# Three in eight dot products of two expert blocks moved from VectorE to GpSimd and ScalarE, in a decoder layer with a product-key expert FFN

## The chip, the cores and the metric

One Trainium2 chip, one core of it. The metric is the device time of one execution of the whole kernel in microseconds.

## The reference

One decoder layer on 1024 tokens of width 1024, in float32. The first part (combined projection, dilated attention, a gated recurrence, cross-attention, gated merge, layer norm) is not touched by the change. The second part is a product-key expert FFN (PEER): each token picks 8 x 16 = 128 of 16384 experts, takes the dot product of its row with each expert's row of `u_tab`, applies GELU and the gate, and sums the experts' rows of `v_tab` with these weights.

```python
q = jnp.einsum('bsd,dk->bsk', h, w_q).reshape(b, s, PEER_HEADS, 2, PEER_DHALF)
sc = jnp.einsum('bshpk,hpnk->bshpn', q, sub_keys).astype(jnp.float32)
...
top, pos = lax.top_k(cand, PEER_TOPK)
idx = jnp.take_along_axis(cidx, pos, axis=-1)
gate = jax.nn.softmax(top, axis=-1)
...
def block(args):
    xt, it, gt = args
    act = jax.nn.gelu(jnp.einsum('td,ted->te', xt, u_tab[it]), approximate=False)
    return jnp.einsum('te,ted->td', gt * act, v_tab[it])
```

Then `h = LN(alpha*h + ffn)`.

## The kernel before

Each engine has its own program, written out by hand in order; semaphores tie them. The tokens are in 8 blocks of 128 (`NBLK`), one token per partition. The dots of block 0 are done earlier, beside the second half of the attention part (`e_rows`, L1766). The stage that the change touches starts at about 1920 us of the span and has these pieces:

- **Gathers.** For block n and slot k (0 to 127), GpSimd waits until the ring slot k mod 8 of `u_ring` is free and issues an indirect DMA of one expert row per token, 512 KB in all (L859).
- **Dots.** `dot(n, k)` on VectorE (L2097) waits for that gather, multiplies the row by the tokens' residual rows, which TensorE has raised into PSUM as `h1_up` (`raise_h1`, L1197), and sums along the row into `coef[:, k]`, in one instruction and an accumulator read. Its semaphore `u_dots` frees the ring slot.
- **Coefficients.** After all 128 dots of a block: `gelus` on ScalarE (L1564), `coefficients` on VectorE (L2105, times the gate), `turn` on TensorE (transpose), `turn_out` on ScalarE.
- **Weights by expert.** For 32 groups of four tokens: `hots` on VectorE (L2080, two comparisons of 128x512 whose operands are both in SBUF), `scale` on ScalarE (four copies), `pair` on TensorE, `pair_out` on ScalarE (into `table`). `hots` may run two groups ahead of `pair`.
- **Values.** `values_of(p, i)` on TensorE (L1215): in pass p, tile i of 64, a tile of 128 rows of `v_tab` (512 KB, a ring of 4 filled from Sync's queue) is multiplied with the table of one or two blocks.

The order: a prologue of 32 sub-steps does `hots(0, sub)` and one dot of block 1 each. Then 9 passes of 64 tiles. In tiles 0 to 27 (`DOT_TILES`) of pass p VectorE does what is left of block p+1's dots, at tile 28 its coefficients, and in tiles 32 to 63 `hots(p+1, ..)` and the first 64 dots of block p+2, two a tile. How many dots stand in a tile is `dots_by` (L511): in pass 0 rows 32 to 127 of block 1 over 28 tiles; in a later pass's first half rows 64 to 127. From tile 16 of pass 0 to tile 15 of pass 1 VectorE also computes the top-k of the last four blocks, one of 64 parts a tile (`topk`, L1662), in front of the tile's dots. Layer norm (`add_rows`, `finish`) is done from pass 2 on with `res2`, which holds the residual rows of the block being finished; `h1` holds the rows that `raise_h1` raises next. Sync's program loads both (`load_h1`).

Of the kernel before, what the change touches and what calls it, by code (L numbers as in the profile page):

```python
# [30 lines left out]
ALU = mybir.AluOpType  # L31
ACT = mybir.ActivationFunctionType
# [6 lines left out]
HALF = 512  # L39
# [10 lines left out]
SLOTS = PH * TOPK  # L50
# [8 lines left out]
NBLK = NHALF * NB  # L59
U_ROWS = 8  # L60
V_TILES = 4
TOK = 4
NTILE = P // 2
NSUB = P // TOK
HALF_T = NTILE // 2
ROWS = 2 * P
DOT_TILES = HALF_T - 4
TURN_TILE = HALF_T - 2
PICK_TILE = HALF_T // 2

E_ROWS = 4
E_GROUPS = SLOTS // E_ROWS
# [125 lines left out]
def layer(nc, A):  # L198
# [21 lines left out]
    h1_d = dram("h1_d", (NHALF * NB, P, D))  # L220
# [4 lines left out]
    with ctx:  # L225
        def sem(name):
            return ctx.enter_context(nc.semaphore(name))
# [21 lines left out]
        ident = at("ident", [P, P])  # L249
# [119 lines left out]
        u_ring = at("u_ring", [P, U_ROWS, D])  # L369
        v_ring = at("v_ring", [P, V_TILES, D])  # L370
        h1 = at("h1", [P, D])
        res2 = at("res2", [P, D])
        g2 = at("g2", [P, D])
        b2 = at("b2", [P, D])
        pidx = [at(f"pidx{i}", [P, SLOTS], U32) for i in range(2)]
# [81 lines left out]
        v_in = [sem(f"v_in{i}") for i in range(V_TILES)]  # L457
        v_used = sem("v_used")
        u_dots, u_gelu, u_coef = sem("u_dots"), sem("u_gelu"), sem("u_coef")
        key_split, key_ready = sem("key_split"), sem("key_ready")  # L460
        hot_one, hot_ready, hot_scaled = sem("hot_one"), sem("hot_ready"), sem("hot_scaled")
        turned, paired, build_out = sem("turned"), sem("paired"), sem("build_out")
# [18 lines left out]

        def dots_before(n, k):
            return SLOTS * (n - 1) + k

        def turn_item(n):

# [55 lines left out]
        def boundary(hf, k):  # L544
            return 2 + 6 * hf + k
# [3 lines left out]
        def _(sp):  # L549
# [198 lines left out]
                sp.dma_start(pgate[n % 2][:, :], gate_d[n]).then_inc(pk_in[n % 2], 16)  # L748

            def load_h1(n):  # L750
                sp.dma_start(h1[:, :], h1_d[n]).then_inc(h1_in, 16)

            def load_values(p, i):

# [11 lines left out]
            for p in range(NBLK + 1):  # L766
                for i in range(NTILE):
                    part = topk_at(NTILE * p + i + 3)
                    if part and part[2] == 0 and part[:2] > (0, 1):
                        load_queries(1, *part[:2])  # L770
                    if p == 0 and i == 4:
                        sp.wait_ge(turned, 1)
                        load_picks(2)
                        sp.wait_ge(h1_raised, 1)
                        load_h1(2)
                        sp.dma_start(res2[:, :], h1_d[0]).then_inc(res2_in, 16)
                    if i == PICK_TILE + HALF_T and p + 3 < NBLK:
                        sp.wait_ge(h1_raised, p + 2)
                        load_h1(p + 3)
                        if p == 1:  # L780
                            sp.wait_ge(tk_out, 32 * NB * 2 + 32)
                            sp.dma_start(g2[:, :], A["ln2_g"].to_broadcast([P, D])).then_inc(par_in, 16)
                            sp.dma_start(b2[:, :], A["ln2_b"].to_broadcast([P, D])).then_inc(par_in, 16)
                        sp.wait_ge(turned, p + 2)
                        load_picks(p + 3)
                    if i == 24 and p >= 2:
                        sp.wait_ge(FV.sem, FV.after("sb", p - 2))
                        sp.dma_start(out_d[0, P * (p - 2):P * (p - 1), :], res2[:, :]).then_inc(p_out, 16)
                    if i == 44 and p >= 2:
                        sp.wait_ge(p_out, 16 * (p - 1))  # L790
                        sp.dma_start(res2[:, :], h1_d[p - 1]).then_inc(res2_in, 16)
                    load_values(p, i)
# [6 lines left out]
        def _(pool):  # L799
# [52 lines left out]
                            u_rows(E_PQ * t // 4, E_PQ * (t + 1) // 4, G_PQ + E_PQ // E_ROWS * e, E_ROWS * G_PQ + E_PQ * e)  # L852

            pool.wait_ge(stage, 3 * boundary(1, 4))
            for n in range(1, NBLK):
                pool.wait_ge(pk_in[n % 2], 32 * (n // 2) + 32)
                for k in range(SLOTS):
                    pool.wait_ge(u_dots, dots_before(n, k) + 1)
                    pool.indirect_dma_start(  # L859
                        out=u_ring[:, k % U_ROWS, :], out_offset=None, in_=u_tab,  # L860
                        in_offset=bass.IndirectOffsetOnAxis(ap=pidx[n % 2][:, k:k + 1], axis=0)).then_inc(u_in[k % U_ROWS], 16)


        @block.tensor
        def _(pe):
# [331 lines left out]
            def raise_h1(n):  # L1197

                pe.wait_ge(h1_in, 16 * n)
                for c in range(2):  # L1200
                    last = pe.matmul(h1_up[:, c, :], ident[:, :], h1[:, HALF * c:HALF * c + HALF], start=True, stop=True)  # L1201
                last.then_inc(h1_raised, 1)

            def pair(n, sub):
# [54 lines left out]
        def _(act):  # L1259
# [303 lines left out]

            def gelus(n):  # L1564
                act.wait_ge(u_dots, dots_before(n + 1, 0) + U_ROWS)
                act.activation(coef[:, :], coef[:, :], ACT.Gelu).then_inc(u_gelu, 1)  # L1566

            def root(n):
                act.wait_ge(FV.sem, FV.after("ep", n))
# [3 lines left out]
            for sub in range(NSUB):  # L1573
                scale(0, sub)
                if sub:
                    pair_out(0, sub - 1)
            for p in range(NBLK + 1):
                for i in range(NTILE):
                    if i == 0 and p < NBLK:
                        pair_out(p, NSUB - 1)  # L1580
                    if i == 4 and p >= 2:
                        root(p - 2)
                    done = NTILE * p + i - TOPK_TILE
                    if done in range(16, 16 * NB + 1, 16):
                        gate_exps(1, done // 16 - 1)
                    if done in range(18, 16 * NB + 3, 16):
                        store_topk(1, done // 16 - 1)
                    if i == DOT_TILES and p + 1 < NBLK:
                        gelus(p + 1)
                    if i == TURN_TILE and p + 1 < NBLK:  # L1590
                        turn_out(p + 1)
                    if i >= HALF_T and p + 1 < NBLK:
                        scale(p + 1, i - HALF_T)
                        if i > HALF_T:
                            pair_out(p + 1, i - HALF_T - 1)
# [4 lines left out]
        def _(dve):  # L1600
# [496 lines left out]
            def dot(n, k):  # L2097

                if k == 0:
                    dve.wait_ge(h1_raised, n)  # L2100
                dve.wait_ge(u_in[k % U_ROWS], 16 * (dots_before(n, k) // U_ROWS) + 16)
                dve.tensor_tensor_reduce(out=u_ring[:, k % U_ROWS, :], in0=u_ring[:, k % U_ROWS, :], in1=h1_up[:, :, :].rearrange("p c n -> p (c n)"),  # L2102
                                         scale=1.0, scalar=0.0, op0=ALU.mult, op1=ALU.add, accum_out=coef[:, k:k + 1]).then_inc(u_dots, 1)

            def coefficients(n):  # L2105
                dve.wait_ge(u_gelu, n)
# [37 lines left out]
            split_keys(0)  # L2144
            for sub in range(NSUB):
                hots(0, sub)
                dot(1, sub)
            for p in range(NBLK + 1):
                for i in range(NTILE):
                    if i >= HALF_T and p + 1 < NBLK:  # L2150
                        hots(p + 1, i - HALF_T)
                    done = NTILE * p + i - TOPK_TILE
                    if done in range(16, 16 * NB + 1, 16):
                        topk_gates(1, done // 16 - 1)
                    part = topk_at(NTILE * p + i)
                    if part:
                        topk(1, *part, score_bank(*part[:2]))
                    if p >= 2:
                        if i == 1:
                            add_rows(p - 2)  # L2160
                        elif i in (3, 4, 7, 8, 9):
                            finish(p - 2, (3, 4, 7, 8, 9).index(i))
                    n = p + 1 + (i >= HALF_T)
                    if n < NBLK and i - NTILE * (i >= HALF_T) < DOT_TILES:
                        now = i - NTILE * (i >= HALF_T)
                        first = SLOTS // 4 if n == 1 and i == 0 else 0 if i == HALF_T else dots_by(n, now - 1)
                        for k in range(first, dots_by(n, now)):
                            dot(n, k)
                    if p + 1 < NBLK:
                        if i == PICK_TILE + 8:  # L2170
                            split_keys(p + 1)
                        if i == DOT_TILES:
                            coefficients(p + 1)
# [22 lines left out]
```

## Time and profile before

| | |
|---|---|
| time, median of 3 runs | 4415.11 us (4405.64 to 4424.81) |
| profiled execution: time, span | 4412.03 us, 4410.2 us |
| TensorE busy (matmuls) | 3790.3 us, 86% |
| VectorE busy | 2714.9 us, 62% |
| GpSimd busy | 1560.0 us, 35% |
| ScalarE busy | 1189.6 us, 27% |
| DMA | 1130.17 MB, mean 256 GB/s |
| dots of L2102 | 896, 1066.2 us busy |
| gathers of L859 | 896, 859.5 us busy on GpSimd, 8.4 us to landing (median) |

The shares are means over the whole span, of stages with different limits. The table of windows below cuts the expert stage at the borders of its pieces. A GpSimd row counts the issue of a gather as busy; the transfer itself is in the DMA share.

### The profile page before, as it was taken

How to read it: one execution, taken by the hardware profiler on the slowest of the kernel's cores; microseconds unless marked ns; L12 is line 12 of the kernel's file. 1: busy time of each engine (PE TensorE's matmuls, PEld its weight loads, DVE VectorE, ACT ScalarE, POOL GpSimd, SP SyncE). 2: the span in 40 equal slices, each digit the busy share in tenths (PEclk: the TensorE clock that was granted, in tenths of full speed). 3: DMA queues.
4: the chain of work that ended last, by engine and by line, in shares of the span. 5: the costliest groups of instructions: out<-in, count | busy, mean ns of one | idle time of the engine just before them, and what ended most of it. 6: DMA issues, size and time to landing. Idle time of an engine off the chain costs nothing.

```text
span 4410.2 us, 45120 instructions
## 1 busy us (share of the span) xinstructions
PE 3790.3 (86%) x14175; PEld 2446.3 (55%) x14175; DVE 2714.9 (62%) x5349; ACT 1189.6 (27%) x2385; POOL 1560.0 (35%) x1317
## 2 busy tenths in 40 slices
PE   7999899798998798675255979899898998989998
PEld 5777777687777676552133435354454544445443
DVE  1555543228877765576999987687786867742000
ACT  1333333223323332251023023041331404224000
POOL 2555444220000376554422354444444444410000
PEclk8999999899999899878577989999999999999999
DMA  7666523364454478699766899999999999963457
GB/s 240 201 209 217 171 82 92 99 205 125 133 154 136 133 243 280 216 319 370 283 221 226 316 371 370 398 369 403 375 384 386 376 407 364 389 261 126 157 172 271
DMA packets 503228, 1130.17 MB, mean 256 GB/s; under 512 B 37836, under 2 KB 249980, under 8 KB 502688
## 3 DMA queue, kind: packets, MB, share of 16 engines
q1 hardware_dynamic: 345248, 575.67, 38.3%
q0 software_dynamic: 147456, 536.94, 32.8%
q10 hardware_dynamic: 10368, 15.73, 1.0%
q8 instruction: 68, 1.11, 0.1%
q14 instruction: 88, 0.72, 0.1%
HBM read 1041.14 MB, written 89.41 MB: 256 GB/s over the span
## 4 chain that ended last, share of the span: by engine, by line
PE 27%; DMA 13%; DVE 13%; issue 3%; POOL 1%; DVEq 0%; ACT 0%
PE ps L1228 23%; DMA u_ring<-in_peer_u,pidx 12%; DVE u_ring L2102 5%; PE ps L1212 4%; DVE hot L2094 1%; DVE hot L2095 1%; DMA v_ring<-in_peer_v 1%; POOL u_ring L859 1%; DVE pick_own L1736 0%; DVE pick_own L1741 0%; DVE got_own L1744 0%; DVE inds_own L1699 0%; DVE inds_own L1687 0%; DVE left_own L1690 0%; PE h_up L1201 0%
## 5 line engine op out<-in xcount | busy, mean ns | idle before, releaser
L1228 PE MATMUL ps<-v_ring,table 128*128 128x512 f32 x4096 | 1841.0, 603 | 24.1 <-DMA v_ring<-in_peer_v 22.8
L1228 PEld LDWEIGHTS ps<-v_ring,table 128*128 128x128 f32 x4096 | 773.1, 194 | 919.3 <-issue 863.6
L859 POOL DMA_INDIRECT u_ring<-in_peer_u,pidx x896 | 859.5, 959 | 1137.9 <-DVE coefe L2102 1075.9
L2102 DVE CUSTOM_DVE_ANT_0 u_ring<-u_ring,h_up 128x1024 f32<-128x1024 f32 x896 | 1066.2, 1216 | 230.7 <-DMA u_ring<-in_peer_u,pidx 220.9
L808 POOL TENSOR_TENSOR w_lo<-w_raw,w_hi 128x1024 fp32r<-128x1024 f32 x200 | 448.0, 2246 | 902.1 <-ACT w_hi L1301 896.8
L918 PE MATMUL ps<-x_hi,w_hi 128*128 128x512 f32 x1280 | 520.8, 407 | 70.7 <-ACT w_hi L1301 62.4
L921 PE MATMUL ps<-x_lo,w_hi 128*128 128x512 f32 x1280 | 507.5, 396 | 0.0
L1212 PEld LDWEIGHTS ps<-hot,hot 128*128 128x128 f32 x2048 | 293.6, 211 | 244.6 <-DVE hot L2095 141.9
L1212 PE MATMUL ps<-hot,hot 128*128 128x128 f32 x2048 | 308.2, 299 | 118.6 <-DVE hot L2095 101.2
L1545 ACT ACTIVATE hot<-hot,by_slot 128x128 f32<-128x128 f32 x1024 | 319.7, 386 | 189.3 <-DVE hot L2094 186.2
L1559 ACT ACTIVATE table<-ps 128x512 f32<-128x512 f32 (+3 forms) x256 | 228.7, 893 | 453.0 <-PE ps L1212 453.0
L918 PEld LDWEIGHTS ps<-x_hi,w_hi 128*128 128x128 f32 x1280 | 246.4, 193 | 138.7 <-ACT w_hi L1301 40.2
L2094 DVE TENSOR_TENSOR hot<-keys,by_slot 128x512 f32<-128x512 f32 x256 | 176.7, 690 | 231.8 <-PE ps L1212 220.8
L927 PE MATMUL ps<-x_hi,w_lo 128*128 128x512 f32 x1280 | 316.5, 389 | 0.2 <-POOL w_lo L808 0.2
L921 PEld LDWEIGHTS ps<-x_lo,w_hi 128*128 128x128 f32 x1280 | 246.0, 192 | 51.9 <-issue 1.9
L927 PEld LDWEIGHTS ps<-x_hi,w_lo 128*128 128x128 f32 x1280 | 240.2, 188 | 50.5 <-POOL w_lo L808 0.6
L1774 DVE CUSTOM_DVE_ANT_0 e_ring<-e_ring,h_up 128x1024 f32<-128x1024 f32 x128 | 155.7, 1221 | 161.4 <-DMA e_ring<-in_peer_u,icole 157.7
L2115 DVE SCALAR_TENSOR_TENSOR res<-res,ps 128x512 f32<-128x512 f32 x16 | 10.3, 684 | 347.7 <-PE ps L1228 347.7
L816 POOL TENSOR_TENSOR w_hi<-w_raw,zero 128x1024 fp32r<-128x1024 f32 x56 | 117.0, 2089 | 248.1 <-PE ps L918 118.3
L1566 ACT ACTIVATE coefe<-coefe 128x128 f32<-128x128 f32 x7 | 2.2, 309 | 746.5 <-DVE coefe L2102 746.5
L2095 DVE TENSOR_TENSOR hot<-keys,by_slot 128x512 f32<-128x512 f32 x256 | 175.1, 684 | 0.0
L1301 ACT ACTIVATE w_hi<-w_raw 128x1024 fp32r<-128x1024 f32 (+1 forms) x144 | 131.9, 916 | 149.4 <-DMA w_raw<-in_w_branch 44.1
(288 smaller groups left out, 3898.7 us busy)
## 6 DMA issues: line engine op xcount, KB each, us to landing
v_ring<-in_peer_v SPq DMA_DIRECT2D x576, 512.0 KB, 6.8
w_raw<-in_w_in SPq DMA_DIRECT2D x104, 512.0 KB, 5.4
wh_d<-w_hi SPq DMA_DIRECT2D x56, 512.0 KB, 2.7
wl_d<-w_lo SPq DMA_DIRECT2D x56, 512.0 KB, 4.2
w_hi<-wh_d SPq DMA_DIRECT2D x56, 512.0 KB, 3.6
w_lo<-wl_d SPq DMA_DIRECT2D x56, 512.0 KB, 3.7
w_raw<-in_w_peer_q SPq DMA_DIRECT2D x32, 512.0 KB, 4.4
u_ring<-in_peer_u,pidx POOLq DMA_INDIRECT x896, 8.4
```

The source lines that it names most:

```text
L808: pool.tensor_tensor(out=w_lo[b][:, 0:k, :], in0=w_raw[b][:, 0:k, :], in1=w_hi[b][:, 0:k, :].bitcast(F32), op=ALU.subtract).then_inc(w_spl ...
L859: pool.indirect_dma_start(out=u_ring[:, k % U_ROWS, :], out_offset=None, in_=u_tab, in_offset=bass.IndirectOffsetOnAxis(ap=pidx[n % 2][:, ...
L918: first = pe.matmul(out, w_hi[b][:, k, :], hi[:, k, :], start=(k == 0), stop=False)
L921: pe.matmul(out, w_hi[b][:, k, :], lo[:, k, :], start=False, stop=False)
L927: last = pe.matmul(out, w_lo[b][:, k, :], hi[:, k, :], start=False, stop=(k == k_n - 1))
L1212: last = pe.matmul(build_bank(item)[:, P * m:P * m + P], hot2[sub % 2][:, m, :], hot1[sub % 2][:, m, :], start=True, stop=True)
L1228: last = pe.matmul(ps[2 * (n % 2) + c][:, :], table[:, row_of(n, i1), :], v_ring[:, j % V_TILES, HALF * c:HALF * c + HALF], start=(n == p ...
L1545: last = act.activation(hot1[sub % 2][:, m, :], hot1[sub % 2][:, m, :], ACT.Copy, scale=by_slot[:, 2, t0 + m:t0 + m + 1])
L1559: last = act.activation(table[:, r0:r0 + near, t0:t0 + TOK].rearrange("p i t -> p t i"), src[:, :, 0:near], ACT.Copy)
L2094: dve.tensor_tensor(out=hot1[sub % 2][:, :, :], in0=numbers(NTILE * (n % 2)), in1=of(0), op=ALU.is_equal).then_inc(hot_one, 1)
L2095: dve.tensor_tensor(out=hot2[sub % 2][:, :, :], in0=numbers(0), in1=of(1), op=ALU.is_equal).then_inc(hot_ready, 1)
L2102: dve.tensor_tensor_reduce(out=u_ring[:, k % U_ROWS, :], in0=u_ring[:, k % U_ROWS, :], in1=h1_up[:, :, :].rearrange("p c n -> p (c n)"), s ...
```

## The change

In blocks 1 and 2 the dots of ring slots 1, 4 and 6 are done in two steps: GpSimd multiplies the gathered row in place by the residual rows in SBUF (`product`), and ScalarE sums it with a copy that accumulates (`sums`). A product stands in GpSimd's program five gathers after its own gather (`POOL_LAG`), and a sum in ScalarE's two tiles after the tile to which the row belongs (`SUM_LAG`). The other five slots stay on VectorE. A gather now waits for whichever of the two semaphores frees its slot, `u_dots` or `u_sums`. Since GpSimd reads the residual rows for longer, block 2's rows are loaded into `res2` instead of `h1`, and the load of `res2` for the first layer norm moves to pass 1. `gelus` also waits for the sums and stands one tile later.

```diff
+POOL_BLOCKS = (1, 2)
+POOL_SLOTS = (1, 4, 6)
+POOL_LAG = 5
+SUM_LAG = 2
...
+        h1_rows = [h1, h1, res2] + [h1] * (NBLK - 3)
...
+        def on_pool(n, k):
+            return n in POOL_BLOCKS and k % U_ROWS in POOL_SLOTS
...
             def load_h1(n):
-                sp.dma_start(h1[:, :], h1_d[n]).then_inc(h1_in, 16)
+                sp.dma_start(h1_rows[n][:, :], h1_d[n]).then_inc(h1_in, 16)
...
                         load_h1(2)
-                        sp.dma_start(res2[:, :], h1_d[0]).then_inc(res2_in, 16)
                     if i == PICK_TILE + HALF_T and p + 3 < NBLK:
                         sp.wait_ge(h1_raised, p + 2)
+                        if p == 0:
+                            sp.wait_ge(u_prods, sums_before(2, 0))
                         load_h1(p + 3)
                         if p == 1:
+                            sp.wait_ge(u_prods, sums_before(3, 0))
+                            sp.dma_start(res2[:, :], h1_d[0]).then_inc(res2_in, 16)
...
+            def product(n, k):
+
+                row = u_ring[:, k % U_ROWS, :]
+                pool.wait_ge(h1_raised, n)
+                pool.wait_ge(u_in[k % U_ROWS], 16 * (rows_before(n, k) // U_ROWS) + 16)
+                pool.tensor_tensor(out=row, in0=row, in1=h1_rows[n][:, :], op=ALU.mult).then_inc(u_prods, 1)
+
             for n in range(1, NBLK):
                 pool.wait_ge(pk_in[n % 2], 32 * (n // 2) + 32)
                 for k in range(SLOTS):
-                    pool.wait_ge(u_dots, dots_before(n, k) + 1)
+                    j = rows_before(n, k)
+                    if j >= U_ROWS:
+                        old = (j - U_ROWS) // SLOTS + 1, (j - U_ROWS) % SLOTS
+                        if on_pool(*old):
+                            pool.wait_ge(u_sums, sums_before(*old) + 1)
+                        else:
+                            pool.wait_ge(u_dots, dots_before(*old) + 1 + U_ROWS)
                     pool.indirect_dma_start(
...
+                    if j >= POOL_LAG:
+                        late = (j - POOL_LAG) // SLOTS + 1, (j - POOL_LAG) % SLOTS
+                        if on_pool(*late):
+                            product(*late)
...
             def gelus(n):
                 act.wait_ge(u_dots, dots_before(n + 1, 0) + U_ROWS)
+                act.wait_ge(u_sums, sums_before(n + 1, 0))
                 act.activation(coef[:, :], coef[:, :], ACT.Gelu).then_inc(u_gelu, 1)
+
+            def sums(n, first, last):
+
+                for k in range(first, last):
+                    if on_pool(n, k):
+                        row = u_ring[:, k % U_ROWS, :]
+                        act.wait_ge(u_prods, sums_before(n, k) + 1)
+                        act.activation(row, row, ACT.Copy, accum_out=coef[:, k:k + 1]).then_inc(u_sums, 1)
...
+                    sums(*rows_at(NTILE * p + i - SUM_LAG))
-                    if i == DOT_TILES and p + 1 < NBLK:
+                    if i == DOT_TILES + SUM_LAG - 1 and p + 1 < NBLK:
                         gelus(p + 1)
...
+            def dots(n, first, last):
+                for k in range(first, last):
+                    if not on_pool(n, k):
+                        dot(n, k)
```

## Rows read from the trace of the kernel before

**Rows 1.** Windows by stage: start:end us, length, busy us (instructions) of each engine, PEclk, DMA share, GB/s.

```profile
1921.00:2000.60 79.60, 57.61 (x251) 48.73 (x252) 74.27 (x126) 68.59 (x187) 42.01 (x39) 0.65 0.89 309
2000.60:2102.30 101.70, 51.01 (x123) 20.56 (x122) 67.89 (x114) 2.81 (x7) 51.78 (x56) 0.82 1.02 396
2102.30:2195.00 92.70, 17.08 (x40) 8.97 (x40) 89.83 (x262) 0.00 (x0) 38.20 (x42) 0.59 0.82 288
...
2210.60:2442.00 231.40, 137.09 (x439) 79.70 (x440) 223.37 (x659) 71.65 (x162) 61.41 (x62) 0.78 0.67 224
2442.00:2545.00 103.00, 103.00 (x265) 47.55 (x264) 99.17 (x311) 0.31 (x1) 34.65 (x37) 1.00 0.93 333
2545.00:2581.30 36.30, 4.36 (x11) 1.62 (x9) 35.58 (x66) 1.62 (x3) 25.95 (x28) 0.63 1.01 391
2855.00:3121.00 266.00, 252.99 (x776) 128.01 (x775) 198.02 (x335) 70.99 (x197) 122.13 (x128) 0.97 1.00 385
```

**Rows 2.** Waits from 2000.6 to 2102.3 us: who waited for what, us, times, longest.

```profile
DVE u_ring L2102 <- DMA u_ring<-in_peer_u,pidx: 33.2, 32, 1.3
```

**Rows 3.** Waits from 2540 to 2590 us.

```profile
PE ps L935 <- DVE coefe L2107: 32.8, 1, 32.8
```

**Rows 4.** Timeline of VectorE in the prologue: start us, us, engine, line, operation.

```profile
1980.65 0.68 DVE L2094 TENSOR_TENSOR hot<-keys,by_slot 128x512 f32<-128x512 f32 x1
...
1981.86 1.20 DVE L2102 CUSTOM_DVE_ANT_0 u_ring<-u_ring,h_up 128x1024 f32<-128x1024 f32 x1
...
1982.99 0.68 DVE L2094 TENSOR_TENSOR hot<-keys,by_slot 128x512 f32<-128x512 f32 x1
```

**Rows 5.** Timeline of ScalarE in the prologue.

```profile
1988.39 1.28 ACT L1545 ACTIVATE hot<-hot,by_slot 128x128 f32<-128x128 f32 x4
...
1989.75 0.87 ACT L1561 ACTIVATE table<-ps 128x384 f32<-128x384 f32 x1
1990.74 1.28 ACT L1545 ACTIVATE hot<-hot,by_slot 128x128 f32<-128x128 f32 x4
```

**Rows 6.** ScalarE groups of 128x1024 copies and of accumulator reads, whole span.

```profile
L1301 ACT ACTIVATE w_hi<-w_raw 128x1024 fp32r<-128x1024 f32 x96 | 101.5, 1057 | 80.4 <-DMA w_raw<-in_w_peer_q 40.3 <-DVEq L533 16.7 <-PE ps L918 6.6
...
L1352 ACT ACTIVATION_READ_ACCUMULATOR prob<-prob,stat 128x1 f32 x96 | 17.9, 187 | 0.0
```

**Rows 7.** GpSimd's two-input and one-input 128x1024 operations: ns min/median/max.

```profile
L808 POOL TENSOR_TENSOR w_lo<-w_raw,w_hi x200: 1272/2398/3803, 78.7 to 1902.0; 128x1024 fp32r<-128x1024 f32 x100
...
L816 POOL TENSOR_TENSOR w_hi<-w_raw,zero x56: 1888/1894/3422, 76.8 to 513.2; 128x1024 fp32r<-128x1024 f32 x56
```

**Rows 8.** Timeline of GpSimd's gather issues from 2108.61 us.

```profile
2108.61 0.94 POOL L859 DMA_INDIRECT u_ring<-in_peer_u,pidx  x1 [0.30 <-issue]
2109.85 0.94 POOL L859 DMA_INDIRECT u_ring<-in_peer_u,pidx  x1 [0.30 <-issue]
```

**Rows 9.** Timeline of GpSimd and VectorE at 1505 and at 1508 us.

```profile
1505.01 2.42 POOL L808 TENSOR_TENSOR w_lo<-w_raw,w_hi 128x1024 fp32r<-128x1024 f32 x1
1505.02 1.22 DVE L1774 CUSTOM_DVE_ANT_0 e_ring<-e_ring,h_up 128x1024 f32<-128x1024 f32 x1 [3.00 <-DMA e_ring<-in_peer_u,icole]
...
1507.59 0.96 POOL L830 DMA_INDIRECT e_ring<-in_peer_u,icole  x1 [0.16 <-issue]
...
1508.56 1.30 POOL L808 TENSOR_TENSOR w_lo<-w_raw,w_hi 128x512 fp32r<-128x512 f32 x1
...
1508.63 1.79 DVE L2013 TENSOR_TENSOR macc<-macc 128x512 f32<-128x512 f32 x1
```

**Rows 10.** Gathers of L859 from 2000.6 to 2102.3 us: issue to landing.

```profile
DMA to landing us min/median/max: 4.9/13.3/19.0
```

**Rows 11.** Gathers of L859 from 2210.6 to 2442 us: issue to landing.

```profile
DMA to landing us min/median/max: 4.2/5.5/8.1
```

**Rows 12.** VectorE groups from 2102.3 to 2545 us: count, busy us, mean ns, idle before.

```profile
L2094 DVE TENSOR_TENSOR hot<-keys,by_slot 128x512 f32<-128x512 f32 x32 | 21.9, 686 | 0.0
...
L1736 DVE TENSOR_TENSOR pick_own<-iota_own,posf_own 128x1024 f32<-128x1024 f32 x16 | 19.8, 1239 | 0.5
```

More of the change, by code:

```diff
@@ L459, in layer @@
         u_dots, u_gelu, u_coef = sem("u_dots"), sem("u_gelu"), sem("u_coef")
+        u_prods, u_sums = sem("u_prods"), sem("u_sums")
         key_split, key_ready = sem("key_split"), sem("key_ready")
@@ L480, in apart, with rows_before, sums_before, rows_at @@
             eng.sem_inc(waited, 1)
-        def dots_before(n, k):
-            return SLOTS * (n - 1) + k
+        def rows_before(n, k):
+            return SLOTS * (n - 1) + k
+        def on_pool(n, k):
+            return n in POOL_BLOCKS and k % U_ROWS in POOL_SLOTS
+        def sums_before(n, k):
+            return sum(on_pool(j // SLOTS + 1, j % SLOTS) for j in range(rows_before(n, k)))
+        def dots_before(n, k):
+            return rows_before(n, k) - sums_before(n, k)
+        def rows_at(step):
+            if step < 0:
+                return 1, step + NSUB, step + NSUB + 1
+            p, i = step // NTILE, step % NTILE
+            n, now = p + 1 + (i >= HALF_T), i - NTILE * (i >= HALF_T)
+            if n >= NBLK or now >= DOT_TILES:
+                return n, 0, 0
+            first = SLOTS // 4 if n == 1 and i == 0 else 0 if i == HALF_T else dots_by(n, now - 1)
+            return n, first, dots_by(n, now)
         def turn_item(n):
@@ L1200, in raise_h1 @@
                 for c in range(2):
-                    last = pe.matmul(h1_up[:, c, :], ident[:, :], h1[:, HALF * c:HALF * c + HALF], start=True, stop=True)
+                    last = pe.matmul(h1_up[:, c, :], ident[:, :], h1_rows[n][:, HALF * c:HALF * c + HALF], start=True, stop=True)
                 last.then_inc(h1_raised, 1)
@@ L1576, in _ @@
                     pair_out(0, sub - 1)
+                if sub >= SUM_LAG:
+                    sums(*rows_at(sub - NSUB - SUM_LAG))
             for p in range(NBLK + 1):
@@ L2100, in dot @@
                     dve.wait_ge(h1_raised, n)
-                dve.wait_ge(u_in[k % U_ROWS], 16 * (dots_before(n, k) // U_ROWS) + 16)
+                dve.wait_ge(u_in[k % U_ROWS], 16 * (rows_before(n, k) // U_ROWS) + 16)
                 dve.tensor_tensor_reduce(out=u_ring[:, k % U_ROWS, :], in0=u_ring[:, k % U_ROWS, :], in1=h1_up[:, :, :].rearrange("p c n -> p (c n)"),
                                          scale=1.0, scalar=0.0, op0=ALU.mult, op1=ALU.add, accum_out=coef[:, k:k + 1]).then_inc(u_dots, 1)
+            def dots(n, first, last):
+                for k in range(first, last):
+                    if not on_pool(n, k):
+                        dot(n, k)
             def coefficients(n):
@@ L2146, in _ @@
                 hots(0, sub)
-                dot(1, sub)
+                dots(*rows_at(sub - NSUB))
             for p in range(NBLK + 1):
@@ L2162, in _ @@
                             finish(p - 2, (3, 4, 7, 8, 9).index(i))
[L2163 to L2168, printed above, removed]
+                    dots(*rows_at(NTILE * p + i))
                     if p + 1 < NBLK:
```

## Prediction

> **What bounds the kernel now.** I read the page's slices first (VectorE at nine tenths only between about 2100 and 2600 us), then cut the expert stage into windows at the places where the program changes what it asks of the engines [rows 1]; the reader should go through that table stage by stage, with the row counts that `dots_by` gives.
>
> - Prologue (1921 to 2000.6): 32 sub-steps, each two `hots` comparisons and one dot. A sub-step takes 2.34 us and VectorE has no gap in it [rows 4]: 1.20 for the two comparisons, 1.14 for a dot. ScalarE has a gap of 0.12 us in the same 2.35 [rows 5], so it is nearly as full.
> - Rows 32 to 86 of block 1 (to 2102.3): DMA share 1.02, and VectorE waits 33 us for gathers [rows 1, 2]. This stage is bound by transfers.
> - Rows 87 to 127 with twelve parts of the top-k (to 2195.0): VectorE is busy 89.8 of 92.7 us.
> - Tiles 28 to 31 have no dots. Then rows 0 to 63 of block 2, with `hots` and top-k (2210.6 to 2442): VectorE 223 of 231 us; and rows 64 to 98 with top-k (to 2545): 99 of 103.
> - Rows 99 to 127 (to 2581.3): both VectorE and the DMAs are full, and TensorE waits 32.8 us for the coefficients [rows 1, 3]. After this each block takes 266 us [rows 1]; that part has no changed dots, so what has been won or lost by the turn of block 2 goes to the end one for one.
>
> So VectorE's time is worth taking away only from 2102 to 2581, and there only while nothing else becomes as slow. GpSimd looks free by its busy share (38 of 93 us in the third window), but a gather costs it more than its 0.94 us: two issues that wait for nothing start 1.24 us apart [rows 8].
>
> **The change part by part.** Ninety-six of 256 dots leave VectorE, at 1.14 us each: 109 us in all, but by stage 12 in the prologue, 36 in the rest of block 1, 24, 13 and 11 in block 2's three stages.
>
> GpSimd's product. The trace has no GpSimd multiply. The nearest rows are its 128x1024 operation with two SBUF tensors, median 2.40, and the one with a broadcast column, 1.89 [rows 7]. The product reads two full tensors, so I take 2.42 [rows 9], and keep 1.89 as the lower end. With the gap of 0.16 to the next issue (1505.01+2.42 to 1507.59 [rows 9]), and less the 0.30 gap that it fills [rows 8], a product adds 2.28 us. A row then costs GpSimd 1.24 + 3/8 x 2.28 = 2.10 us. The Trainium skill (GPSIMD Engine Reference, section 3.1) measures 4497 ns for a two-input operation of 2048 elements on GpSimd against 2293 on VectorE, and advises against such work there; half of it, 2.25, is an estimate near the row's 2.40, and by it the sum below would be about 8 us lower.
>
> ScalarE's sum: copies of this size take 1.06 and an accumulator read 0.19 [rows 6], so 1.06 to 1.25; I take 1.15 in a full stage and 1.25 as a latency.
>
> Prologue: ScalarE gets 12 x 1.15 = 13.8 us and has 31 x 0.12 = 3.7 to spare: **+10 us**. VectorE's 12 dots less buy nothing there, since `hots` runs at most two sub-steps ahead of ScalarE.
>
> Block 1 to its coefficients. Row 31's dot starts at 2000.6, so the gather of row 39, which takes its slot, is issued at 2002.1 now and at 2012 then. From it to the gather of row 127 there are 88 steps: 88 x 2.10 = 185, to 2197. While value tiles stream (some 24 rows) I add 4 us, because a product sits behind six issues on GpSimd's own queue and waits for a landing: in 9.7 us of issues and products a gather of 5.5 us [rows 11] has landed, one of 13.3 [rows 10] has not; with at most six rows in flight I take 11. I add 6 us in the top-k stage, where VectorE frees slots in bursts and GpSimd waits for its reads (below): 2207. Then come row 127's issue, those of rows 128 to 131 and the products of rows 124 and 126 (10.6 us), and a sum (1.25): 2219. The coefficients now stand at 2198, after one part of the top-k. **+21, the prologue's 10 within it.** All that VectorE saves here is lost, since the dots were not what came last any more.
>
> The shared access. At 1508.56 GpSimd starts a two-tensor operation of 1.30 us, and VectorE's addition of two SBUF tensors, begun 0.07 later, takes 1.79, while such an operation takes 0.69 alone; a dot, which reads one operand in PSUM, takes its 1.22 beside a product-like operation [rows 9, 12]. So `hots` and the top-k's selections can be held, dots cannot. In rows 0 to 63 of block 2 a tile will take about 6.4 us. A product is running when the first comparison comes in 2.42/6.4 = 0.38 of cases, for 1.21 more on average: 0.46. In 0.6/6.4 it asks during the first and goes ahead of the second: 0.23. For the selections (1.24 us twice in four tiles, and one of 0.69) I get 0.40 in the same way. That is 1.1 us of each product against 1.14 saved: 24 x 0.04, **-1**. The ends are 0 and 2.42 a product: -27 to +31. Rows 64 to 98 have no `hots`: 13 x (1.14 - 0.40): **-10**.
>
> Rows 99 to 127. The first gather issued here is row 107's, 1.5 us in; 20 steps x 2.10 = 42; the same 11.9 us to the last sum: 55.4 for 36.3, **+19**. No cover: TensorE is waiting.
>
> Moved work. Block 2's residual rows load into `res2` where `h1` stood, and the load of `res2` for the first sum goes from tile 4 of pass 0 to tile 48 of pass 1, behind GpSimd's 96 products. Sync's queue has value tiles behind that wait, but the products are done by tile 28; and `add_rows` needs `res2` 17 tiles later, while gathers of the same size land in 19.0 us at most [rows 10]. Zero, unless the products slip by a whole half pass. `gelus` goes a tile later in ScalarE's program, where nothing stands before it in first halves: zero.
>
> Sum: +21 - 1 - 10 + 19 = +29. The profiled execution took 4412.0 (span 4410.2), so 4441; the median of the runs shown is 3 higher: **4444 us**.
>
> **Rivals.** *Losses and gains cancel.* Same mechanism, softer: no extra waits in block 1 (+11 there), 0.5 us held per product (-15, -8), tail +17: +5, 4420. For it: where the DMAs aren't full, gathers land in 5.5 us [rows 11], so GpSimd may never wait. Against: it needs every in-order wait to vanish.
>
> *Faster.* The product costs GpSimd 1.89, as with one tensor read, and holds nobody. A step is 1.90: rows to 127 at 2012 + 167 + 11 = 2190, so -5; then -27, -15, and a tail of 1.5 + 38 + 10.8 - 36.3 = +14: -33, 4382. It decides from a step of about 2.0 us down with under 0.5 held. For it: VectorE is full for 480 us. Against: the median of 2.40 [rows 7], and the addition at 1508.
>
> *Every product holds a comparison.* Products follow issues, which follow freed slots, so they could fall on `hots` each time: 24 x (2.42 - 1.14) = +31 for -1: +61, 4476. It makes things slower from 1.14 us held per product up. The Trainium skill (SBUF — State Buffer, "SBUF: two separate sides") says of this pair of ports that whichever of a two-SBUF-input VectorE operation and a GpSimd operation starts first has it for the whole instruction, and the other blocks. By that rule, the trace agrees at 1508; how often they meet it doesn't say.
>
> **How the numbers follow.** Chances: my sum 0.45 (own range 4425 to 4462), cancelling 0.25, faster 0.15, held comparisons 0.15. Half a percent is 22 us, about what a measurement can tell: 4393 and 4437. Slower: 0.32 of my sum's 0.45, and 0.15, and a little: 0.48. Same: 0.13 + 0.23 = 0.36. Faster: 0.16. The range 4392 to 4485 leaves out most of the faster case and what lies above the held one.
>
> **What would show it.** Right: GpSimd busy without waits on dots in rows 39 to 127 and 107 to 127, products of 2.4, ScalarE without gaps in a longer prologue, VectorE waiting for the Gelu of block 1, comparisons with a maximum over 2 us. Wrong: products under 2 us; VectorE still full to 2195 with an early turn; comparisons all at 0.69; or a block period other than 266 us afterwards.

## The result and the profile after

The changed kernel took 4471.02 us (median of 4 runs, 4462.45 to 4473.26) against 4413.25 us for the one before in the same session (4405.64 to 4424.81): a ratio of 1.0118, 95% interval 1.0098 to 1.0138. The profiled span is 4471.5 us for 4410.2, 61.3 us more. The sign and the wide range of the prediction (4392 to 4485) held, but the range it gave its own sum (4425 to 4462) did not: that sum was half of what came, +29 forecast, +52 in the stages that it covers. The other 9.3 us of the two spans are 7.6 from a later start of the expert stage, where the code is the same (over the fourteen profiles of this study it starts between 1912 and 1938 us, in no visible relation to what was changed), and 1.7 behind it.

VectorE's timeline gives the borders of each stage: the first `hots`; the start of the 32nd; the first `MAX8` of the top-k; the coefficients of block 1; the start of the last `hots` of the 32 that stand beside rows 0 to 63 of block 2; the end of the last top-k part; the coefficients of block 2. The sum includes 2.0 us to the next `hots`.

| stage, us | before | after | difference | forecast |
|---|---|---|---|---|
| prologue, rows 0 to 31 of block 1 | 78.4 | 97.6 | +19.2 | +10 |
| rows 32 to 86 | 102.9 | 119.5 | +16.6 | } +11 |
| rows 87 to 127, to the coefficients | 95.8 | 100.5 | +4.7 | |
| turn, then rows 0 to 63 of block 2 with `hots` and top-k | 238.1 | 230.6 | -7.5 | -1 |
| rows 64 to 98 with top-k | 108.7 | 101.4 | -7.3 | -10 |
| rows 99 to 127, to the coefficients | 36.7 | 63.0 | +26.3 | +19 |
| sum | 662.5 | 714.5 | +52.0 | +29 |

From there to the end it is 1826.6 us before and 1828.3 after: what is lost by the turn of block 2 goes to the end one for one. The windows of the kernel after, with the columns of [rows 1]:

```profile
1928.70:2026.30 97.60, 64.52 (x244) 54.33 (x244) 87.55 (x101) 73.74 (x200) 66.06 (x47) 0.52 0.70 229
2026.30:2145.80 119.50, 57.74 (x128) 24.97 (x128) 46.41 (x74) 28.68 (x55) 97.76 (x74) 0.74 0.92 342
2145.80:2246.30 100.50, 17.09 (x40) 8.95 (x40) 88.01 (x252) 19.85 (x35) 86.45 (x64) 0.58 0.82 280
...
2476.80:2578.20 101.40, 99.27 (x257) 46.41 (x258) 97.33 (x293) 19.48 (x35) 66.99 (x50) 0.98 0.91 341
2578.20:2641.20 63.00, 11.84 (x28) 4.94 (x26) 26.03 (x44) 15.58 (x27) 53.72 (x41) 0.61 0.80 269
```

Read the fifth and the third of the busy columns (GpSimd, VectorE) together. In the second and last windows VectorE is busy 46 of 119 us and 26 of 63, while GpSimd is busy 98 and 54: the bound has moved to GpSimd. In the prologue VectorE is busy 88 of 98 us although 12 of its 32 dots are gone. The groups of the expert stage (1920 to 2650 us) say why:

```profile
L890 POOL TENSOR_TENSOR u_ring<-u_ring,h 128x1024 f32<-128x1024 f32 x48 | 114.3, 2381 | 8.0 <-DMA u_ring<-in_peer_u,pidx 7.1
...
L1622 ACT ACTIVATE u_ring<-u_ring 128x1024 f32<-128x1024 f32 x96 | 101.3, 1055 | 277.5 <-POOL u_ring L890 277.5
...
L2153 DVE TENSOR_TENSOR hot<-keys,by_slot 128x512 f32<-128x512 f32 x66 | 74.3, 1125 | 7.1 <-PE ps L1259 3.8 <-ACT by_slot L1585 3.3
L2154 DVE TENSOR_TENSOR hot<-keys,by_slot 128x512 f32<-128x512 f32 x66 | 65.1, 986 | 0.0
```

Products cost 2.38 us and sums 1.055, near the forecast. The comparisons, 0.686 us in [rows 12], now have means of 1.125 and 0.986. Durations over the plain one add up to 30.3 us in the prologue (the twelfth product falls on its border; 27.7 us lie before it) and 18.9 in rows 0 to 63 of block 2. Below, a VectorE operation is called held when it takes longer than its plain duration while a product runs. One place of the prologue, first VectorE's timeline, then GpSimd's:

```profile
1994.64 0.68 DVE L2154 TENSOR_TENSOR hot<-keys,by_slot 128x512 f32<-128x512 f32 x1
1995.86 0.70 DVE L2153 TENSOR_TENSOR hot<-keys,by_slot 128x512 f32<-128x512 f32 x1 [0.55 <-PE ps L1259]
1996.48 3.24 DVE L2154 TENSOR_TENSOR hot<-keys,by_slot 128x512 f32<-128x512 f32 x1
1999.64 1.21 DVE L2161 CUSTOM_DVE_ANT_0 u_ring<-u_ring,h_up 128x1024 f32<-128x1024 f32 x1
```

```profile
1995.84 0.93 POOL L902 DMA_INDIRECT u_ring<-in_peer_u,pidx  x1 [2.66 <-ACT u_ring L1622]
1996.78 2.38 POOL L890 TENSOR_TENSOR u_ring<-u_ring,h 128x1024 f32<-128x1024 f32 x1
1999.32 1.25 POOL L902 DMA_INDIRECT u_ring<-in_peer_u,pidx  x1 [0.16 <-issue]
```

The product runs from 1996.78 to 1999.16 in its usual time; the comparison ends at 1999.72, 0.56 later. All 27 held comparisons end 0.55 or 0.56 us after the product that they met. Dots stay at 1.21 beside products, as forecast from [rows 9].

### The profile page after: what moved, and what is told of

It is laid out like the page before. It is cut to its first block, busy times and chain, and to the rows that moved or that the text cites. A ratio compares the mean times of both kernels' runs of the same rounds, so it can differ in the third digit from the quotient of the medians.

```text
span 4471.5 us, 45320 instructions
## 1 busy us (share of the span) xinstructions
PE 3810.5 (85%) x14175; PEld 2462.4 (55%) x14175; DVE 2678.1 (60%) x5157; ACT 1290.5 (29%) x2577; POOL 1794.3 (40%) x1413
## 4 chain that ended last, share of the span: by engine, by line
PE 29%; issue 21%; DMA 13%; DVE 11%; POOL 7%; POOLq 0%; ACT 0%; DVEq 0%; SPq 0%; ACTq 0%
PE ps L1275 23%; DMA u_ring<-in_peer_u,pidx 10%; PE ps L1259 4%; DVE u_ring L2161 3%; POOL u_ring L902 2%; POOL e_ring L860 2%; POOL u_ring L890 1%; DMA e_ring<-in_peer_u,icole 1%; POOL w_lo L838 1%; DVE hot L2153 1%; DVE hot L2154 1%; DMA v_ring<-in_peer_v 1%; PE ps L965 1%; PE ps L968 1%; PE ps L974 1%
## 5 line engine op out<-in xcount | busy, mean ns | idle before, releaser
L2161 DVE CUSTOM_DVE_ANT_0 u_ring<-u_ring,h_up 128x1024 f32<-128x1024 f32 x800 | 955.2, 1217 | 310.8 <-DMA u_ring<-in_peer_u,pidx 295.6
L965 PE MATMUL ps<-x_hi,w_hi 128*128 128x512 f32 x1280 | 523.0, 409 | 66.3 <-ACT w_hi L1348 58.1
L1259 PE MATMUL ps<-hot,hot 128*128 128x128 f32 x2048 | 317.4, 305 | 124.1 <-DVE hot L2154 114.8
L2153 DVE TENSOR_TENSOR hot<-keys,by_slot 128x512 f32<-128x512 f32 x256 | 205.8, 804 | 236.7 <-PE ps L1259 181.4
L2154 DVE TENSOR_TENSOR hot<-keys,by_slot 128x512 f32<-128x512 f32 x256 | 195.2, 763 | 0.0
L1622 ACT ACTIVATE u_ring<-u_ring 128x1024 f32<-128x1024 f32 x96 | 101.3, 1055 | 277.5 <-POOL u_ring L890 277.5
```

Of the source, the lines that this page charges most:

```text
L965: first = pe.matmul(out, w_hi[b][:, k, :], hi[:, k, :], start=(k == 0), stop=False)
L1259: last = pe.matmul(build_bank(item)[:, P * m:P * m + P], hot2[sub % 2][:, m, :], hot1[sub % 2][:, m, :], start=True, stop=True)
L2153: dve.tensor_tensor(out=hot1[sub % 2][:, :, :], in0=numbers(NTILE * (n % 2)), in1=of(0), op=ALU.is_equal).then_inc(hot_one, 1)
L2154: dve.tensor_tensor(out=hot2[sub % 2][:, :, :], in0=numbers(0), in1=of(1), op=ALU.is_equal).then_inc(hot_ready, 1)
```

## The experiments

The theory: the change costs time in two ways of about equal size, GpSimd's order of gathers and products (2.10 us a row), and VectorE instructions held while a product runs. The rivals: ScalarE's sums set the pace (my prologue step), or waits for landings do. Stages below are named by the table's order, one to six.

**No body of the offload.** The products are left out, and the sum reads one column.

```diff
                         if on_pool(*late):
-                            product(*late)
+                            pass
...
-                        act.activation(row, row, ACT.Copy, accum_out=coef[:, k:k + 1]).then_inc(u_sums, 1)
+                        act.activation(coef[:, k:k + 1], row[:, 0:1], ACT.Copy).then_inc(u_sums, 1)
```

> Leaves out the work of the 96 moved dots: GpSimd makes no product and ScalarE copies one column of the row instead of summing it, so the gathers and the ring stay, and only VectorE's relief is left. Before 4413, changed kernel 4471. Theory A (GpSimd's 2.1 us a row and its hold on VectorE's comparisons are the cost): the relief itself is real where VectorE was full, 15 dots of 1.14 us in rows 87 to 127, 24 and 13 in block 2, and little in the prologue and where the DMAs are full: about -60, 4353. Theory C (VectorE's relief is worth nothing, transfers and the ring bind anyway): 4413.

Measured: 4377.54 us, ratio 0.9911 (0.9885 to 0.9937). The stages sum to 608.9 us for 662.5: 72.7, 107.1, 78.7, 212.0, 92.6, 43.8. The relief of VectorE alone is worth 54 us in these stages, half of the 109 us of dots taken away. It is earned in stages three to five (59.3 us) and in the prologue (5.7); stages two and six become 4.2 and 7.1 us longer, where the DMA share is 1.00, so an earlier arrival meets the transfers. The time fell by 37 us only (60 were expected): in this profile the expert stage starts 16.9 us later than before.

**ScalarE's sums, no product.** As above, but with the whole copy that accumulates.

> Leaves out GpSimd's products; ScalarE sums the raw rows, so its load and its place in the ring are those of the changed kernel. Theory A: the time of the kernel without both, plus about 10 us in the prologue where ScalarE becomes the slowest: 4363. Theory B (ScalarE's sums, late in its program, free the ring slots too late and are the main cost): stays above 4440.

Measured: 4380.69 us, 0.991 (0.9879 to 0.9942). Stages 84.0, 108.0, 78.7, 211.5, 92.7, 45.4, sum 622.3. The sums cost 11.3 us in the prologue and 2 elsewhere. The prologue is still only 5.6 us longer than before the change, not 10. The time is 18 us above the 4363 expected and far below theory B.

**The products, no sums.**

```diff
-                        act.activation(row, row, ACT.Copy, accum_out=coef[:, k:k + 1]).then_inc(u_sums, 1)
+                        act.activation(coef[:, k:k + 1], row[:, 0:1], ACT.Copy).then_inc(u_sums, 1)
```

> Keeps GpSimd's products and replaces ScalarE's sum by a copy of one column at the same place (the sums are left out). Theory A: the changed kernel less some 8 us of the prologue and less 1 us of the latency behind each last product: about 4460. Theory B: back to about 4413.

Measured: 4462.76 us, 1.0106 (1.008 to 1.0132). The prologue takes 100.7 us, with 30.9 us of held comparisons: ScalarE was not what made it long, and the 8 us expected from it did not come. The time is near the 4460 expected, but that is luck. The fourth stage is the surprise, 216.8 us for the changed kernel's 230.6. There 7 comparisons are held for 5.9 us in all, where the changed kernel has 15 held for 18.9. The sums themselves don't cost these 14 us (they cost nothing in this stage without products, the experiment before); they free the slots later, and the products meet the comparisons at other moments.

**GpSimd busy as long, without reading SBUF.** The product becomes two fills (0.97 and 0.95 us in the trace), then three (0.31 more, and the waits between them).

```diff
-                pool.tensor_tensor(out=row, in0=row, in1=h1_rows[n][:, :], op=ALU.mult).then_inc(u_prods, 1)
+                pool.memset(row, 0.0).then_inc(u_half, 1)
+                pool.wait_ge(u_half, 2 * sums_before(n, k) + 1)
+                pool.memset(row, 0.0).then_inc(u_half, 1)
+                pool.wait_ge(u_half, 2 * sums_before(n, k) + 2)
+                pool.memset(u_ring[:, k % U_ROWS, 0:256], 0.0).then_inc(u_prods, 1)
```

> GpSimd writes the row twice with zeros, one fill after the other, instead of multiplying it (the product is left out), so it is busy at the same places but reads nothing from SBUF. Theory A, part on the shared read access: comparisons return to 0.69 us at most, and with fills of about 1.2 us each the time falls by the held time that lay on the path, 20 to 35 us of the 49 us that the comparisons lost in the changed kernel: 4436 to 4451. If GpSimd's time alone matters and the hold doesn't: 4471. With shorter fills it falls further, by 0.375 times the missing time a row where GpSimd binds.

> GpSimd fills the row with zeros in three pieces that together take as long as a product, about 2.4 us, and reads nothing from SBUF (the product is left out). The two-piece fill, 1.9 us, gave 4410. Theory A with the hold: comparisons at 0.69, and only the 0.4 us a fill come back where GpSimd binds: 88 rows x 0.15 in block 1 and some 3 us in the last stage of block 2, so 4425 to 4430; what is left to the 4471 of the changed kernel, some 44 us, is the hold. If the length of GpSimd's work was all and the hold nothing: 4471.

Measured: two fills 4409.96 us, 0.9987 (0.9972 to 1.0003), sum of stages 645.5; three fills 4430.59 us, 1.0024 (1.0011 to 1.0036), sum 666.1: 81.1, 118.0, 96.2, 211.1, 95.3, 62.4. The fills were shorter than the 1.2 us that the first expectation took, so its 4436 to 4451 did not come; the second, 4425 to 4430, did. A third fill of 0.3 us and its wait cost 21 us over the 96 rows. Three fills take 2.34 us (median) for a product's 2.36, and from the gather of row 39 to that of row 127 it takes 190.5 us, for 191.1 with products: GpSimd's work is as long as in the change. With three fills the groups of the comparisons from 1937 to 2650 us are back at the plain durations:

```profile
L2158 DVE TENSOR_TENSOR hot<-keys,by_slot 128x512 f32<-128x512 f32 x75 | 51.7, 689 | 24.4 <-PE ps L1264 21.0 <-ACT by_slot L1590 3.3
L2159 DVE TENSOR_TENSOR hot<-keys,by_slot 128x512 f32<-128x512 f32 x75 | 51.3, 684 | 0.0
```

So a GpSimd of this length that holds no comparison leaves the change worth next to nothing either way (+3.6 us in the stages). Differences of neighbouring kernels split the +52 (they are steps in one order, one profile each). "Time on GpSimd" is not free of holding: fills hold no comparison, but small VectorE operations, for 5.8, 6.4 and 3.3 us in stages three, five and six.

| stage | relief of VectorE | sums on ScalarE | time on GpSimd | read by the product | all |
|---|---|---|---|---|---|
| one | -5.7 | +11.3 | -2.9 | +16.5 | +19.2 |
| two | +4.2 | +0.9 | +10.0 | +1.5 | +16.6 |
| three | -17.1 | 0.0 | +17.5 | +4.3 | +4.7 |
| four | -26.1 | -0.5 | -0.4 | +19.5 | -7.5 |
| five | -16.1 | +0.1 | +2.6 | +6.1 | -7.3 |
| six | +7.1 | +1.6 | +17.0 | +0.6 | +26.3 |
| sum | -53.6 | +13.4 | +43.8 | +48.4 | +52.0 |

**Only where VectorE is full.** The whole computation, with fewer rows offloaded: those that stand beside the top-k, of block 1 rows 84 to 115, of block 2 rows 0 to 91; then the same without rows 0 to 63 of block 2, where `hots` runs; then only rows 0 to 31 of block 1.

```diff
-            return n in POOL_BLOCKS and k % U_ROWS in POOL_SLOTS
+            return k % U_ROWS in POOL_SLOTS and ((n == 1 and 84 <= k < 116) or (n == 2 and k < 92))
```

> The change only for rows that lie beside the top-k: rows 84 to 115 of block 1 and 0 to 91 of block 2 (12 and 34 dots moved); the prologue, the transfer-bound stage and the last stage keep all dots on VectorE. Full computation. In the changed kernel the two middle stages of block 2 were 7.5 and 7.3 us shorter; with 8 us in block 1 and no late products before the two turns: about -20, 4393. If the hold by the products eats the relief in all these stages: 4413.

> As the kernel before it, but also without the rows that lie beside the comparisons: rows 84 to 115 of block 1 and 64 to 91 of block 2 (12 and 10 dots moved). Full computation. 22 dots of 1.14 us less 0.3 to 0.4 us held each: about -17, 4396. It tells whether the 24 dots beside the comparisons earn anything: if not, this is as fast as the kernel with them.

> The change only in the prologue: rows 0 to 31 of block 1 (12 dots moved). Full computation. My working of before had it +10 (ScalarE the slowest); the trace of the changed kernel has the prologue 19 us longer, with comparisons of 3.2 us. If this is the hold it shows here too: the prologue 19 us longer, the total 4425 to 4432, less where the transfer-bound stage behind it takes some of it in.

Measured: 4411.79 us, 0.9979 (0.9968 to 0.999); 4423.42 us, 1.0006 (0.9992 to 1.0019); 4453.72 us, 1.0083 (1.0059 to 1.0108). The first is faster than before by 0.2% (20 us were expected, 9 came), with a sum of stages of 650.8: 78.9, 102.2, 94.8, 230.6, 103.9, 38.4. Its fourth stage has the same 18.8 us of held comparisons as the changed kernel, against 24 dots (27.4 us) taken away, and gains 7.5. Without those rows nothing is left (sum 662.3 for 662.5; 17 us were expected): the whole gain is that of the 24 dots beside the comparisons, and the 22 dots of stages three and five alone earn nothing. The last gives the prologue's price alone: 17.8 us there (19 expected), and 8.2 more in the stage after it, where the wait for transfers might have absorbed it and did not. The gather of row 39 comes 106.4 us after the first `hots` (81.1 before), and the 88 steps from it to row 127 take 176.2 us (175.2 before), so a late start only moves them. Between the prologue's border and that gather stand the twelfth held comparison (2.5 us) and a wait of 3.66 us of GpSimd for a sum.

**Shorter products.** The rows of the first of these three, each product in four pieces of 256 columns or two of 512, and the four pieces in the whole change.

```diff
-                pool.tensor_tensor(out=row, in0=row, in1=h1_rows[n][:, :], op=ALU.mult).then_inc(u_prods, 1)
+                for c in range(4):
+                    part = slice(D // 4 * c, D // 4 * (c + 1))
+                    last = pool.tensor_tensor(out=row[:, part], in0=row[:, part], in1=h1_rows[n][:, part], op=ALU.mult)
+                last.then_inc(u_prods, 1)
```

> The whole computation, with GpSimd's products limited to rows 84 to 115 of block 1 and 0 to 91 of block 2, each product issued as four pieces of 256 columns. Theory (a VectorE comparison is held by the GpSimd instruction that it meets, until that instruction ends): the hold shrinks from up to 2.4 us to one piece, some 0.7 us, so comparisons stay under about 1.6 us, and the stage falls from 651 us with whole products to about 640: ratio about 0.9955. Rival (the hold lasts as long as GpSimd's work as a whole, or each piece takes a new hold): comparisons as before in sum, the extra fixed cost of three pieces a product on top: ratio 1.000 or above.

> As the kernel with quarters, but each product in two pieces of 512 columns. Theory: holds of at most some 1.3 us, stage about 645 us, ratio about 0.9965. Rival: no better than whole products, 0.998.

> The whole change (three in eight rows of all of blocks 1 and 2), each product in four pieces of 256 columns. Theory: the 48 us of held comparisons shrink to about 15, while each product costs GpSimd some 0.6 us more, that is 0.22 us a row, about 25 us over the stages where its order of gathers sets the pace: 4455 to 4465 us, slightly under the changed kernel's 4471. Rival (hold not by instruction): 4490 or more.

Measured: quarters 4408.09 us, 0.9972 (0.9959 to 0.9986), sum of stages 653.8; halves 4413.34 us, 0.9987 (0.9974 to 0.9999), sum 657.2; the whole change in quarters 4477.67 us, 1.0131 (1.01 to 1.0163), sum 726.8. None of the three times forecast by the theory came, and cutting the product buys nothing that the measurement can tell: the quarters' stages take 3.0 us more than with whole products, the halves' 6.4, those of the whole change in quarters 12.3. The rivals had this right, though not their numbers for the quarters (1.000 or above, 4490 or more). With halves 15 comparisons are held for up to 2.64 us, each to about 0.55 us after the end of the second half, as if the product were one instruction. With quarters nine of the prologue's comparisons wait for all four pieces, 3.64 or 3.65 us each; VectorE's timeline and GpSimd's in the whole change:

```profile
1967.01 3.65 DVE L2157 TENSOR_TENSOR hot<-keys,by_slot 128x512 f32<-128x512 f32 x1
```

```profile
1967.33 2.78 POOL L892 TENSOR_TENSOR u_ring<-u_ring,h 128x256 f32<-128x256 f32 x4
```

and in block 2 both sides give way in turn; the same two engines of the kernel with fewer rows:

```profile
2303.55 1.23 DVE L2156 TENSOR_TENSOR hot<-keys,by_slot 128x512 f32<-128x512 f32 x1
2304.71 1.21 DVE L2157 TENSOR_TENSOR hot<-keys,by_slot 128x512 f32<-128x512 f32 x1
```

```profile
2303.43 3.75 POOL L892 TENSOR_TENSOR u_ring<-u_ring,res 128x256 f32<-128x256 f32 x4
```

No comparison there exceeds 1.23 us, but 41 are longer than 0.8 and the four pieces take up to 3.75 us for 2.77 undisturbed. The total of held time is 17.3 us, with whole products 18.8. GpSimd's step rises to 204.3 / 88 = 2.32 us a row in the whole change, for 2.17 with whole products. Why four pieces are sometimes interleaved and two never were stays open.

**The sums ahead of the gate's exponentials.**

```diff
+                    sums(*rows_at(NTILE * p + i - SUM_LAG))
...
-                    sums(*rows_at(NTILE * p + i - SUM_LAG))
```

> The whole change, with ScalarE's sums put ahead of the gate's exponentials in each step of the loop, so that they don't stand behind an exponential that waits for VectorE. Theory: the 6.1 us that GpSimd's gather waits for a sum at the start of the last stretch goes, the stretch from the end of the zone to the last coefficients falls from 63 to about 57 us, the rest is unchanged: about 4466 us. Rival (the gathers' landing and the row pace set this stretch anyway): no change.

Measured: 4466.05 us, 1.0121 (1.0092 to 1.0151), in a session where the kernel before took 4419.49; the total can't tell it from the changed kernel (1.0118), and that it is the 4466 expected is luck. The last stage takes 58.1 us for 63.0 (57 forecast), and the sum of stages is 711.6 for 714.5. But the mechanism was only half hit: a sum still stands behind an exponential; GpSimd's wait there is 2.14 us, by the trace for a dot, where it was 6.10 for a sum. ScalarE's and GpSimd's timelines:

```profile
2563.30 0.31 ACT L1352 ACTIVATE gex_own<-gex_own 128x128 f32<-128x128 f32 x1 [10.78 <-DVE gex_own L1811]
2563.51 1.04 ACT L1622 ACTIVATE u_ring<-u_ring 128x1024 f32<-128x1024 f32 x1
...
2564.67 0.94 POOL L902 DMA_INDIRECT u_ring<-in_peer_u,pidx  x1 [2.14 <-DVE coefe L2161]
```

## Why the prediction was right in sign and short in size

**GpSimd's step: right.** The gather of row 39 is issued at 2038.72 and that of row 127 at 2229.80: 191.1 us over 88 steps, 2.17 each, where I had 185 and 10 for waits. Eight rows that wait for nothing take 16.75 us, 2.09 each. GpSimd's timeline shows two or three issues and a product in turn:

```profile
2035.25 0.94 POOL L902 DMA_INDIRECT u_ring<-in_peer_u,pidx  x1 [3.66 <-ACT u_ring L1622]
2036.20 2.35 POOL L890 TENSOR_TENSOR u_ring<-u_ring,h 128x1024 f32<-128x1024 f32 x1
2038.72 0.98 POOL L902 DMA_INDIRECT u_ring<-in_peer_u,pidx  x1 [0.16 <-issue]
...
2042.19 2.35 POOL L890 TENSOR_TENSOR u_ring<-u_ring,h 128x1024 f32<-128x1024 f32 x1
2044.71 0.98 POOL L902 DMA_INDIRECT u_ring<-in_peer_u,pidx  x1 [0.16 <-issue]
2045.99 0.94 POOL L902 DMA_INDIRECT u_ring<-in_peer_u,pidx  x1 [0.30 <-issue]
2046.95 2.36 POOL L890 TENSOR_TENSOR u_ring<-u_ring,h 128x1024 f32<-128x1024 f32 x1
...
2229.80 0.98 POOL L902 DMA_INDIRECT u_ring<-in_peer_u,pidx  x1 [0.16 <-issue]
```

The three-fill kernel gives this mechanism without held comparisons: +43.8 us. Of the waits that I added between rows 39 and 127, the 4 us for landings came (three products wait 4.8 us in all), the 6 us for bursts hardly: some 2 us are left for them.

**Prologue: the failed step, in cause and size.** I wrote "ScalarE gets 12 x 1.15 = 13.8 us and has 31 x 0.12 = 3.7 to spare: +10 us", and that VectorE's dots buy nothing there. The whole sums alone lengthen it by 5.6 us; leaving them out of the change leaves it at 100.7. VectorE sets it: 78.4 us, less 12 x 1.14 = 13.7 for the dots, plus 27.7 of held comparisons, 3.8 of waits for TensorE and 1.2 more for the first landing is 97.4, for 97.6 measured. VectorE's dots do buy something there: with their relief alone the prologue is 5.7 us shorter. That my +10 has the sign of the +19 measured is luck, since its cause was not what set the time. In the sum I had priced held comparisons only in block 2, though [rows 4] show two comparisons in each 2.34 us of the prologue.

**To the coefficients of block 1: +40.4 measured, +21 forecast.** Nearly all of the 19 us missed lie ahead of the gather of row 39, which comes 28.9 us later than before from the first `hots` on, where I had 10. Nine of them are the prologue's. The rest is the twelfth held comparison (2.5 us), the wait for a sum at the gather of row 38 (3.66) and the product behind it (2.5 with its gap), the last two in the lines above. The steps between rows 39 and 127 took 4 us less than I gave them. The last sum ends 12.1 us after the gather of row 127, for 11.9 forecast, but the coefficients come 4.3 us later still: 1.3 until VectorE's last dot, and 3.0 for the Gelu with a top-k part that stands before them. I had put nothing between, and in the three-fill kernel that is nearly so: the coefficients come 12.7 us after that gather. In the changed kernel VectorE is late, with small operations held that I had not priced, 12.0 us in rows 87 to 127. VectorE's timeline of the kernel after:

```profile
2215.61 3.00 DVE L2135 TENSOR_SCALAR key_u<-pidx 128x128 uint32<-128x128 uint32 x1
...
2221.12 2.22 DVE L1761 CAST indf_own<-inds_own 128x64 f32<-128x64 uint32 x1
...
2232.82 2.87 DVE L1789 TENSOR_SCALAR posu_own<-pos_own 128x32 uint32<-128x32 uint32 x1
```

Such operations take 0.2 to 0.3 us in this stage before. They end 0.05 to 0.10 us after the product beside them. In the three-fill kernel the same casts have means up to 0.90 us and end 0.05 us after a fill, so fills hold these too, one fill at a time.

**Rows 0 to 63 of block 2: -7.5 for -1.** Here a product costs VectorE less than it gives. 24 dots less are 27.4 us, the hold 18.9: 0.79 us a product for my 1.1, of which the comparisons are more than I reckoned (0.79 for 0.69) and the selections of 1024 columns less (0 for 0.40). How much is held depends on when they meet: without the sums it was 5.9 us.

**Rows 64 to 98: -7.3 for -10.** Near; 13 dots less are 14.8 us, and small operations are held for 8.8 us (the split above has 6.1 more than with fills, which hold such operations too). The two comparisons that fall in this stage aren't held.

**Tail: +26.3 for +19.** The step held: 20 steps from the gather of row 107 take 43.0 us for 42. But that gather comes 6.6 us into the stage, not 1.5, since GpSimd's first gather in it, of row 105, waits for a sum that ScalarE has behind an exponential, whose input VectorE delivers late. ScalarE's and GpSimd's timelines:

```profile
2578.41 0.31 ACT L1352 ACTIVATE gex_own<-gex_own 128x128 f32<-128x128 f32 x1 [14.78 <-DVE gex_own L1811]
2578.62 1.04 ACT L1622 ACTIVATE u_ring<-u_ring 128x1024 f32<-128x1024 f32 x1
2579.57 0.19 ACT L1622 ACTIVATION_READ_ACCUMULATOR u_ring<-u_ring 128x1 f32 x1
2580.02 0.94 POOL L902 DMA_INDIRECT u_ring<-in_peer_u,pidx  x1 [6.10 <-ACT u_ring L1622]
```

The last sum ends 11.8 us after the gather of row 127, for 11.9 forecast. Between it and the Gelu stands a load of ScalarE's function table, which I had not counted. The kernel before did it at 2549.15, ahead of a wait of 30.8 us for the dots; now the sums stand in front of it:

```profile
2639.58 1.28 ACT L1614 ACT_TABLE_LOAD   x1
2640.88 0.31 ACT L1614 ACTIVATE coefe<-coefe 128x128 f32<-128x128 f32 x1
2641.22 0.29 DVE L2171 TENSOR_TENSOR coefe<-coefe,pgate 128x128 f32<-128x128 f32 x1 [7.71 <-ACT coefe L1614]
```

TensorE's wait for the coefficients, 32.8 us in [rows 3], is 51.7 here.

**The rivals.** The measured time is 5 us from "every product holds a comparison" (4476), but by another way: that rival put +31 into rows 0 to 63 of block 2, which gained. The products did fall on `hots` each time, in the prologue, where all 12 held one for 30.3 us. "Losses and gains cancel" (+5) fell on the waits, which did not vanish, and on holds; only its time is near that of the kernel with three fills (+9.5), which makes no product. "Faster" fell on its first condition, a product of 1.89: it is 2.36 to 2.38. Its -5 for block 1 also doesn't follow from its own figures, which give 2190 for 2198, -8.

## What to carry to other kernels

Only half of the busy time taken from VectorE was worth anything, even with nothing in its place, since two of the six stages wait for transfers and the prologue gave back only 5.7 of 13.7 us. Offload where the relieved engine is what the stage waits for (here 0.2% faster with rows beside the top-k, where the whole change cost 1.2%), and test each such stage: stages three and five alone gave nothing. Before moving elementwise work to GpSimd, list what VectorE does beside it in every stage, small casts and scalar operations too, and price each meeting up to the full length of the GpSimd instruction. In an in-order engine that issues gathers, each microsecond of other work per row is paid on every row once that engine is the slowest.

## What the runs showed of the hardware that was not expected

- The comparison that starts first is not safe. Eleven comparisons of the kernel after began 0.29 to 0.31 us before a product and were all held to its end (3.23 or 3.24 us), while the product took its usual 2.37. Without the sums one that began 0.57 us before a product was held too (3.49). One that began 0.22 us before a product kept its 0.69, and the product took 2.69. So the order of the starts in the trace does not tell who waits. The page "SBUF — State Buffer" of the Trainium skill ("SBUF: two separate sides") gives the pair to whichever starts first, for the whole instruction; the whole-instruction part agrees with these rows, the order as the trace shows it does not.
- Small operations of 32 to 128 columns (casts, `TENSOR_SCALAR`) were held up to 3.00 us beside products, and up to 1.60 us in the three-fill kernel, where comparisons kept a mean of 0.69.
- A hold is not confined to one instruction: two pieces held each comparison to the end of the second. Four pieces can give way to a comparison and lose about a microsecond doing so (3.75 for 2.77); two pieces never did.
